# Gate columns of the mLSTM group as eight extra columns of its value projection, and small passes moved between VectorE, ScalarE and GpSimd

## The reference, cut to what matters

```python
# mLSTM: 4 gates of each kind are columns 1280..1287 of w_in
q, k, v, o, i_pre, f_pre = split_cols(p, (GW, GW, GW, GW, nh, nh))
log_i = gate(i_pre, i_bias)
bcum  = cumsum(log_sigmoid(gate(f_pre, f_bias)))
# S5: complex diagonal state, per state p
mag, ang = exp(lr * step), li * step
ab_re, ab_im = mag * cos(ang), mag * sin(ang)
den   = lr * lr + li * li
co_re = ((ab_re - 1.0) * lr + ab_im * li) / den
co_im = (ab_im * lr - (ab_re - 1.0) * li) / den
# RWKV-7: key scaled by its gate
k = k * (1.0 + (a - 1.0) * k_a)
```

## Time and profile before

| | |
|---|---|
| median of 3 runs | 480.02 us |
| the profiled execution: its time, and its span from first to last instruction | 479.55 us, 477.7 us |
| PE busy | 467.7 us, 98% |
| DVE busy | 345.0 us, 72% |
| ACT busy | 272.5 us, 57% |
| POOL busy | 108.4 us, 23% |
| mean granted TensorE clock | 0.997 |
| DVE busy from 60 to 120 us | 58.7 us |
| first read of `xres` (DVE, L2146) | 211.2 us |
| weight load, median from issue to landing | 4.8 us |

### The profile page before, as it was taken

One profiled execution on the slowest core, in us unless ns is written; L12 is line 12 of the kernel. 1 busy time (PEld: TensorE's weight loads), 2 busy tenths in 40 slices (PEclk: granted clock), 3 DMA queues, 4 the chain that ended last, 5 costly groups with the idle time before them and its releaser, 6 DMA issues.

```text
span 477.7 us, 8231 instructions
## 1 busy us (share of the span) xinstructions
PE 467.7 (98%) x3330; PEld 407.4 (85%) x3330; DVE 345.0 (72%) x482; ACT 272.5 (57%) x448; POOL 108.4 (23%) x75
## 2 busy tenths in 40 slices
PE   9999999999999999999999999999999999999995
PEld 6999888988889887889998887888888888888884
DVE  3999999999789987887564747766767777642234
ACT  5778884426334557589366657555555555553332
POOL 0005327793566610000000000000000000444450
PEclk9999999999999999999999999999999999999998
DMA  7884428221411226274633622565554555455502
GB/s 268 331 326 158 173 89 325 69 95 55 149 56 54 90 89 263 90 263 165 233 101 145 238 91 88 184 227 197 206 200 177 176 185 189 169 206 213 185 0 89
DMA packets 12697, 78.91 MB, mean 165 GB/s; under 512 B 1487, under 2 KB 2164, under 8 KB 4084
## 3 DMA queue, kind: packets, MB, share of 16 engines
q1 hardware_dynamic: 12660, 78.39, 45.4%
HBM read 77.33 MB, written 1.84 MB: 166 GB/s over the span
## 4 chain that ended last, share of the span: by engine, by line
PE 74%; DVE 4%; issue 0%; DVEq 0%; ACT 0%
PE bank L415 73%; DVE h L1956 1%; DVE wm_rest L386 1%; DVE wk_rest L386 0%; PE bank L943 0%; PE bank L974 0%; DVE arena L1978 0%; PE bank L653 0%; DVE arena L1899 0%; DVE arena L1969 0%; DVE arena L1979 0%; DVE arena L1927 0%; DVE arena L1925 0%; DVE arena L1898 0%; DVE xres L2146 0%
## 5 line engine op out<-in xcount | busy, mean ns | idle before, releaser
L415 PE MATMUL bank<-h,w_high 128*128 128x512 f32 (+1 forms) x392 | 120.7, 373 | 0.0
L380 ACT ACTIVATE w_high<-ring 128x1024 fp32r<-128x1024 f32 x63 | 66.2, 1058 | 61.2 <-PE bank L415 57.0
L386 DVE TENSOR_TENSOR w_rest<-ring,w_high 128x1024 fp32r<-128x1024 f32 x51 | 63.2, 1245 | 48.8 <-ACT w_high L380 48.6
L415 PE MATMUL bank<-h,w_rest 128*128 128x256 f32 x320 | 89.6, 280 | 0.0
L415 PEld LDWEIGHTS bank<-h,w_high 128*128 128x128 f32 x392 | 68.8, 188 | 13.6 <-issue 0.5
L386 POOL TENSOR_TENSOR w_rest<-ring,w_high 128x1024 fp32r<-128x1024 f32 x7 | 16.8, 2400 | 256.5 <-ACT w_high L380 256.5
L415 PEld LDWEIGHTS bank<-h,w_rest 128*128 128x128 f32 x320 | 60.5, 189 | 0.0
L386 DVE TENSOR_TENSOR w_rest<-third_slot,w_high 128x1024 fp32r<-128x1024 f32 x27 | 32.7, 1223 | 27.3 <-ACT w_high L380 27.2
L415 PE MATMUL bank<-arena 64*64 64x64 f32 (+6 forms) x786 | 50.2, 253 | 2.2 <-POOL arena L1116 1.1
L415 PEld LDWEIGHTS bank<-arena 64*64 64x64 f32 (+3 forms) x786 | 41.8, 144 | 11.3 <-issue 4.6
L415 PE MATMUL bank<-h,we_high 128*128 128x256 f32 x256 | 47.2, 287 | 1.2 <-DVE we_rest L386 0.8
(11 more groups left out here) (346 smaller groups left out, 1038.7 us busy)
## 6 DMA issues: line engine op xcount, KB each, us to landing
ring<-weights SPq DMA_DIRECT2D x49, 1024.0 KB, 4.8
third_slot<-weights SPq DMA_DIRECT2D x15, 1024.0 KB, 4.8
gain<-gains SPq DMA_DIRECT2D x3, 512.0 KB, 5.8
cst<-consts SPq DMA_DIRECT2D x1, 1216.0 KB, 8.6
par<-params SPq DMA_DIRECT2D x1, 1168.0 KB, 10.6
kx<-x_t SPq DMA_DIRECT2D x2, 512.0 KB, 5.7
ring<-weights SPq DMA_DIRECT2D x2, 512.0 KB, 6.6
vx<-mem_t SPq DMA_DIRECT2D x1, 1024.0 KB, 10.0
```

The costliest lines, as they stand in the source:

```text
L380: nc.scalar.activation(split_half(i)[0], raw_half(i), ACT.Copy).then_inc(S["w_high"], 1)
L386: e.tensor_tensor(rest_, raw_half(i), high.bitcast(F32), ALU.subtract).then_inc(rest_done(i)[0], 1)
L415: return nc.tensor.matmul(out_, lhsT, rhs, start=start, stop=stop, skip_group_check=True)
```

## The change

- **Gates.** `w_gate` shrinks from 36 to 8 columns per tile. Buffer pairs `we2` and `we3` are 264 columns wide; their last 8 columns hold the split gate weights, made once by two small ACT operations (high) and two small DVE operations (rest). ml_v's two token halves go to banks 6 and 2 with 264 columns each; ACT's `gated_values` copies 8 gate columns and 256 values of each, scaled. PE transposes the gate columns (two transposes into bank 7) between the two halves of ml_o, after waiting until ACT has moved both. The float32 products, L1793 and the gates' `x_scale` go.
- **Phases.** The eight first passes move from DVE to ACT, in groups of 3, 3 and 2 among the highs. `highs(9)` comes ahead of the table load, `highs(15)` ahead of the next one; `rests(9)` comes ahead of the subtraction L1782, `rests(15)` ahead of `conv_back` of ml_q.
- **S5 coefficients** go to POOL, ahead of `s5_readout`; the denominator and its reciprocal stay on DVE, earlier.
- **Key scale** `Kh` (L1854) and **nM** (L1947) move from DVE to ACT.
- **Banks and buffers.** ml_o uses bank 0; the A products' banks are reordered (the last in bank 0, no bank twice); BKt and Vt swap places. The second `prs` lies on `xres`, so `rotate_back(1)` no longer waits for `h_rest`, and the load of `xres` moves from slot 12 to slot 22, after `s5_y`.

```diff
-GATES = 36
+GATES = 2 * NH
+GATE_ROWS = 36
-        prs = [v4(pr_, 2, T), v4(flat(vx), 2, T)]
+        prs = [v4(pr_, 2, T), v4(flat(xres), 2, T)]
+        gate_cols = v3(R_[:, 0:2 * 64], 64)
-            w_early = [pair(stage, f"we{i}", HALF, 256) for i in range(HALF_BUFS)]
+            w_early = [pair(stage, f"we{i}", HALF, 256) for i in range(2)]
+            w_gated = [pair(stage, f"we{i}", 4 * (256 + GATES), 256 + GATES) for i in range(2, HALF_BUFS)]
+            w_early += [[x[:, :, 0:256] for x in w] for w in w_gated]
@@ tensor
+            def values_and_gates(n, names, banks, act):
+                for name, b in zip(names, banks):
+                    pe_open(pe, name, b)
+                pe.wait_ge(S["gate_split"], 4)
+                for j in range(2):
+                    i = 2 * n + j
+                    wait_rest(pe, i)
+                    for m in range(2):
+                        o = bank[banks[m]][:, 0:256 + GATES]
+                        for k in range(4):
+                            kt = 4 * j + k
+                            last = mm3(o, [x[:, kt, m * P:(m + 1) * P] for x in act],
+                                       [x[:, k, :] for x in w_gated[j]], kt == 0, kt == KD - 1)
+                        if j == 1 and m == 0:
+                            last.then_inc(full[banks[0]], 1)
+                    used(last, i, names[1] if j else None)
-            o = pe_open(pe, "gates", 2)
-            pe.wait_ge(S["gate_gain"], 1)
-            for k in range(KD):
-                last = mm(o[0:GATES, 0:T], v3(prm("w_gate"), GATES)[:, k, :], hT[:, k, :], k == 0, k == KD - 1)
-            last.then_inc(full[2], 1)
-            split_values(7, "ml_v", 0, h_split)
-            split_channel_major(8, "ml_o", 1, h_split)
+            values_and_gates(7, ("ml_v0", "ml_v1"), (6, 2), h_split)
+            split_channel_major(8, "ml_o", 0, h_split, None, (0,))
+            o = pe_open(pe, "gates", 7)
+            moved(pe, "ml_v0")
+            moved(pe, "ml_v1")
+            for m in range(2):
+                last = nc.tensor.transpose(o[0:GATE_ROWS, m * P:(m + 1) * P], gate_cols[:, m, 0:GATE_ROWS], const("ident"))
+            last.then_inc(full[7], 1)
+            split_channel_major(8, "ml_o", 0, h_split, None, (1,))
-                    b = (4, 5, 6, 7, 0, 2, 3, 6)[i]
+                    b = (4, 5, 1, 7, 6, 2, 3, 0)[i]
@@ sync
+                if n == S_V6:
+                    wait_full(sp, "s5_y")
                     sp.dma_start(xres, x_rows.rearrange("(m p) c -> p m c", p=P)).then_inc(S["xres_in"], 16)
@@ gpsimd
+            s5_coefficients()
             s5_readout()
-                if q == 1:
-                    pool.wait_ge(S["h_rest"], 4)
@@ scalar
+            def gated_values(m, name):
+                o = wait_full(act, name)
+                act.wait_ge(S["rstd_col"], 1)
+                act.wait_ge(S["zeros_ready"], 2)
+                a.activation(v3(gate_cols[:, m, :], 32)[:, :, 0:NH], v3(o[:, 256:256 + GATES], NH), ACT.Copy,
+                             scale=rstd_col[:, m:m + 1])
+                a.activation(mlv[:, m, :], o[:, 0:256], ACT.Copy, scale=rstd_col[:, m:m + 1]).then_inc(free_of(name), 1)
+            def phase(i):
+                a.activation(sin[:, i, :], const("time"), ACT.Copy, scale=frac[:, i:i + 1]).then_inc(S["phase"], 1)
+            for i in range(3):
+                phase(i)
             highs(7)
             shifted("rw_k", 1)
             highs(8)
+            for i in range(3, 6):
+                phase(i)
+            highs(9)
+            for i in range(6, 8):
+                phase(i)
+            for j in range(2):
+                a.activation(w_gated[j][0][:, :, 256:256 + GATES], raw_gates(j), ACT.Copy).then_inc(S["gate_split"], 1)
+            highs(15)
+            moved(act, "rw_a")
+            for j in range(2):
+                e = a.activation(Kh[:, j, :], ab[:, j, :], ACT.Identity, bias=one_ka[:, j:j + 1], scale=half_ka[:, j:j + 1])
             highs(H_MID + 2)
             act.wait_ge(S["rw_E"], 1)
-            project_values("ml_v", mlv)
+            gated_values(0, "ml_v0")
+            gated_values(1, "ml_v1")
+            o = wait_full(act, "gates")
-            act.wait_ge(S["ml_rows"], 3)
+            act.wait_ge(S["ml_row_step"], 3)
+            a.activation(rows[2][0:NH, :], rows[0][0:NH, :], ACT.Copy, scale=-1.0).then_inc(S["ml_rows"], 1)
@@ vector
-            for i in range(8):
-                last = v.tensor_scalar(sin[:, i, :], const("time"), frac[:, i:i + 1], None, ALU.mult)
-            last.then_inc(S["theta"], 1)
+            rests(9)
+            dve.wait_ge(S["phase"], 8)
             v.scalar_tensor_tensor(sin, cos, ROUND, sin, ALU.subtract, ALU.subtract).then_inc(S["theta"], 1)
-            rests(9)
-            v.tensor_tensor(w_gate, w_gate, spread(prm("pre_mix"), GATES), ALU.mult).then_inc(S["gate_gain"], 1)
+            for j in range(2):
+                dve.wait_ge(S["gate_split"], j + 1)
+                high, rest_ = (x[:, :, 256:256 + GATES] for x in w_gated[j])
+                v.tensor_tensor(rest_, raw_gates(j), high.bitcast(F32), ALU.subtract).then_inc(S["gate_split"], 1)
+            rests(15)
-            for j in range(2):
-                last = v.tensor_scalar(Kh[:, j, :], ab[:, j, :], half_ka[:, j:j + 1], one_ka[:, j:j + 1], ALU.mult, ALU.add)
-            x_scale("gates", GATES, 1)
-            v.tensor_scalar(nM, lf, -1.0, None, ALU.mult).then_inc(S["ml_rows"], 1)
```

More of the change, by code:

```diff
@@ L320, in wait_slot @@
             return slot(n)
-        SCALED = ["rw_wag", "rw_k", "rw_r", "rw_v", "ml_q", "ml_k", "gates", "ml_o"]
+        SCALED = ["rw_wag", "rw_k", "rw_r", "rw_v", "ml_q", "ml_k", "ml_o"]
         def scaled(eng, name):
@@ L844, in _ @@
             moved(pe, "qk3")
-            moved(pe, "ml_v")
+            moved(pe, "ml_v1")
             attend("num", 2, mlv, E)
@@ L1132, in s5_readout, with s5_coefficients @@
                 g.tensor_scalar(c_im, xr, -1.0, None, ALU.mult).then_inc(S["s5_c"], 1)
+            def s5_coefficients():
+                lr, li, cos1, sin1 = prm("lam_re"), prm("lam_im"), cos[:, :, 1], sin[:, :, 1]
+                pool.wait_ge(S["sincos"], 3)
+                pool.wait_ge(S["s5_step"], 2)
+                g.tensor_tensor(s8b, mag, cos1, ALU.mult)
+                g.tensor_tensor(s8c, mag, sin1, ALU.mult).then_inc(S["s5_co_step"], 1)
+                pool.wait_ge(S["s5_co_step"], 2)
+                g.tensor_scalar(s8b, s8b, -1.0, None, ALU.add).then_inc(S["s5_co_step"], 1)
+                pool.wait_ge(S["s5_co_step"], 3)
+                g.tensor_tensor(co_re, s8b, lr, ALU.mult)
+                g.tensor_tensor(s8a, s8c, li, ALU.mult)
+                g.tensor_tensor(co_im, s8c, lr, ALU.mult)
+                g.tensor_tensor(frn, s8b, li, ALU.mult).then_inc(S["s5_co_step"], 1)
+                pool.wait_ge(S["s5_co_step"], 4)
+                g.tensor_tensor(co_re, co_re, s8a, ALU.add)
+                g.tensor_tensor(co_im, co_im, frn, ALU.subtract).then_inc(S["s5_co_step"], 1)
+                pool.wait_ge(S["s5_co_step"], 5)
+                pool.wait_ge(S["s5_den"], 2)
+                g.tensor_tensor(co_re, co_re, den8, ALU.mult)
+                g.tensor_tensor(co_im, co_im, den8, ALU.mult).then_inc(S["s5_co"], 1)
             pool.wait_ge(S["sq_m_ready"], 1)
             sum_tiles(pool, g, sq_m, "mem_summed")
+            s5_coefficients()
             s5_readout()
@@ L1364, in _ @@
             a.activation(rwE[:, 2], Gp, ACT.Exp, scale=-1.0).then_inc(S["rw_E"], 1)
[L1365 to L1368, removed]
             s5_driving(0)
@@ L1373, in _ @@
             act.wait_ge(S["rw_E"], 1)
-            project_values("ml_v", mlv)
+            gated_values(0, "ml_v0")
+            gated_values(1, "ml_v1")
+            o = wait_full(act, "gates")
+            a.activation(rows[0][0:NH, :], o[32:32 + NH, 0:T], ACT.Identity,
+                         bias=prm("f_bias", NH)).then_inc(S["ml_gate"], 1)
+            a.activation(rows[1][0:NH, :], o[0:NH, 0:T], ACT.Identity, bias=prm("i_bias", NH)).then_inc(free_of("gates"), 1)
             act.wait_ge(S["ml_gate"], 1)
@@ L1739, in _ @@
             dve.wait_ge(S["theta"], 3)
+            lr, li = prm("lam_re"), prm("lam_im")
+            v.tensor_tensor(den8, lr, lr, ALU.mult)
+            v.tensor_tensor(s8b, li, li, ALU.mult).then_inc(S["s5_den"], 1)
+            dve.wait_ge(S["s5_den"], 1)
+            v.tensor_tensor(den8, den8, s8b, ALU.add).then_inc(S["s5_co_step"], 1)
+            dve.wait_ge(S["s5_co_step"], 1)
+            v.reciprocal(den8, den8).then_inc(S["s5_den"], 1)
             def mix(n, name):
@@ L1776, in _ @@
             rests(8)
+            dve.wait_ge(S["consts_in"], 16)
             for i in range(8):
@@ L1852, in _ @@
             k2 = rwM[:, 2:4, :]
-            for j in range(2):
-                last = v.tensor_scalar(Kh[:, j, :], ab[:, j, :], half_ka[:, j:j + 1], one_ka[:, j:j + 1], ALU.mult, ALU.add)
```

(7 more changed lines are left out.)

53 lines of the change are left out of this document (18 added, 35 removed).

## The result

The changed kernel takes 484.44 us (median of 5 runs; 484.03 for the four without the one named below) against 479.83 us of the kernel before on the same chip, a ratio of 1.0088 for those four (95% interval 1.0073 to 1.0103). On a second chip it was 484.01 against 479.77, 1.0082 (1.0065 to 1.0099). Forecast were 475.9 us and a range of 473.6 to 478.8. One profiled execution of the changed kernel took 1174 us, with TensorE's products at about twice their time (776 instead of 379 ns for those of h with `w_high`); it is left out, and all that follows reads the ordinary execution of the second chip (484.17 us, span 482.4).

What follows compares the result with a forecast made beforehand. The prediction took PE, busy 467.7 of 477.7 us, as the bound. Its terms, 0.2 + 3.1 + 0.4 - 0.7 + 0.3 + 1.1 - 1.0 + 0.7 = 4.1 us less, gave 475.9 us, range 473.6 to 478.8.

Steps and rivals of the forecast that it cites:

- The collision, -1.0: Before 119.40 us, freed `rotate_back(1)` on POOL runs beside DVE's memory rests 4 to 7 and costs 1.0 us.
- the alternating lock: Rival with a late slot 9: POOL-DVE collision costs 2.5, transposes wait 1.5; 1.8 us less, 478.2 us; chance 0.20.
- The issue before level five, +0.7: At 125.37 us PE waits for POOL's mask; made some 4 us early, it ends that wait and gains 0.7 us.
- Gates, +3.1: PE's float32 gate products go, 3.58 us, less 0.2 for 264-column products and 0.3 for transposes: 3.1 us gained.
- The wait at the transposes, -0.7: Near 67 us PE waits for ACT's `gated_values`, held by slot 9's landing and highs: 0.7 us lost.
- ACT from 22 to 50 us, +0.2: ACT's idle time takes most of the phase passes, gate splits and `Kh`; of half 8's 0.8 us gap 0.2 is kept.
- ml_o's bank, +0.4: At 68 us PE's wait for the bank that ml_k holds goes, since ml_o uses bank 0: 0.4 us gained.
- the last A bank, +0.3: At 78 us PE's wait before the last A product goes, since no bank is used twice: 0.3 us gained.
- DVE after ml_k, "3.4 us sooner": Without `Kh` and the gates' scale on DVE, `rw_tilde` comes about 3.4 us sooner and keeps up with PE.
- nM, +1.1: nM leaves DVE for ACT: 1.19 us less 0.1 of overlap, so DVE gains 1.1 and is 4.4 ahead at 113 us.
- the five kinds of wait: PE's waits from 20 to 180 us, given as 3.3 us together; with 0.7 of issue, 4.0 us of gaps.
- the rival in which all gaps close: No wait at the transposes and no collision: 7.1 us less at most, 473.3 to 474.5 us; chance 0.14.

Runs made afterwards that it cites:

- b3_both: The changed kernel with 224 unused columns behind the parameters (addresses of before) and the `h_rest` wait of `rotate_back(1)` put back; 477.80 us, ratio 0.9955.
- b1_pad: The changed kernel with 224 unused columns behind the parameters, so later buffers lie at their addresses of before; 481.46 us, ratio 1.0032.
- b2_h_rest: The changed kernel with only the wait of `rotate_back(1)` for `h_rest` put back; 479.67 us, ratio 0.9999.
- d4_phases_dve: b3_both with the eight first phase passes back on DVE; 478.34 us, ratio 0.9972.
- d2_free_rotation: The kernel before with `rotate_back(1)` freed of its `h_rest` wait, the second `prs` on `xres` and its later load, nothing else; 484.21 us, ratio 1.0093.
- d3: b3_both with POOL's mask of level five ahead of `rotate_back(1)` instead of behind it; 477.83 us, ratio 0.9961.
- f1: The changed kernel padded, level-four mask behind memory rests 0 to 3, level-five mask behind rests 4 to 7 and ahead of `rotate_back(1)`; 477.73 us, ratio 0.9958.
- a1_after: The changed kernel once more, unchanged; 484.01 us, ratio 1.0082.

## Why the prediction was wrong

It failed at one term that was mis-sized, "I take 1.0" for what `rotate_back(1)` meets (3.4 us, and 1.28 us of clock behind it), and at one that it lacked, the addresses (2.0 us). Without the two (b3_both) the change gains 2.2 us by the ratio, 1.7 by the spans (476.0 against 477.7). The forecast's own terms for such a kernel, without the collision and with the issue back, come to 4.1 + 1.0 - 0.7 = 4.4, so the remaining ones were too high as well. Point by point, on b3_both where not said otherwise:

- **The collision, -1.0 (bounds 0 to 3.5).** The mechanism was named and the place was right; the size was 3.4 us on DVE (5.08 - 1.66), the upper bound. That the sum of five times 0.7 comes so near is luck: four operations met POOL, and three of them lost 1.0 us each and the last 0.4. "Back-to-back DVE operations mostly keep going once started" did not hold here. The 0.7 us of the earlier trace rows was one meeting, and I multiplied it by an uncertain share of five operations; what counts is how often the two engines meet, and which of them has to wait. Here it was DVE, with operations (474 ns) far shorter than POOL's (1.3 us alone). The same meeting went the other way at 101 us in the kernel before, where three long DVE operations with operands in SBUF alone kept their 1.21 us and POOL's product beside them took 5.39; its timeline, POOL and then DVE (the first of the three is in the earlier trace rows):

```profile
101.42 5.39 POOL L1149 TENSOR_TENSOR arena<-arena 128x512 f32<-128x512 f32 x1
...
103.31 1.21 DVE L386 TENSOR_TENSOR wk_rest<-ring,wk_high 128x1024 fp32r<-128x1024 f32 x1
104.44 1.21 DVE L1969 SCALAR_TENSOR_TENSOR arena<-arena 128x1024 f32<-128x1024 f32 x1
```

  What decides between the two ways is not shown. The Trainium skill ("SBUF — State Buffer", SBUF: two separate sides) says that such operations exclude each other for the whole instruction. This trace agrees: the level updates, with one operand in a bank of PSUM, kept their 0.40 us beside POOL at 114 us, and the memory rests, with SBUF operands alone, did not. The half's rest at 115.14, two SBUF inputs as well, kept its 1.22 us, and there it was POOL's product that took 2.25.
- **What the wait does to PE's clock.** No term. A wait of 3.70 us brought 1.2 GHz behind it and 1.28 us more (1.05 in b1_pad, where the products took 56.77). A much shorter one can do it too: in b2_h_rest and in d4_phases_dve the clock fell at 112.0 us, behind waits of 1.39 and 1.37 us, and in b3_both, behind the same 1.39, it did not. Windows of b2_h_rest and then of b3_both:

```profile
112.00:114.00 2.00, 2.00 (x12) 2.00 (x11) 2.00 (x6) 0.00 (x0) 0.00 (x0) 0.50 0.00 0
```

```profile
112.00:114.00 2.00, 2.00 (x19) 2.00 (x18) 2.00 (x5) 0.00 (x0) 0.00 (x0) 1.00 0.00 0
```

  There it cost little, since the waits of 0.27 and 0.71 us behind it closed. What decides whether it falls is open. The rival "the alternating lock" priced the collision at 2.5; by itself, with the clock, it is 4.5 (d2_free_rotation).
- **The issue before level five, +0.7.** Right in the changed kernel, where it went, paid for by the collision. In b3_both it is back (0.71). The mask and the memory rests want POOL and DVE at one time; d3 and f1 show that either order costs about the same.
- **Addresses, no term.** 2.0 us. The diff shows the constant `GATES` shrink a parameter block at the front of memory; that everything behind it moves was to be seen, that it has a price was not to be had from any row of before.
- **Gates, +3.1.** Right on PE. Products of 264 columns last 286 and 282 ns (high and rest) against 285 and 283 for 256 columns, and from the first start of ml_v's 48 to the last it is 5.77 us (59.56 to 65.33 in a1_after) against 5.72 (61.76 to 67.48 before), so my 0.2 for them is nearer 0. No float32 product of 36 rows is left.
- **The wait at the transposes, -0.7.** Measured 0.61 in a1_after, 0.50 in b3_both. The size was right and the reason half: slot 9 was issued at 61.10 instead of 61.55, not at 59.7, and PE came later too. The rows of PE's waits before 80 us, timeline of b3_both:

```profile
10.37 0.51 PE L423 MATMUL bank<-h,we_high 128*128 128x256 f32 x2 [0.74 <-DVE we_rest L394]
...
38.65 0.51 PE L423 MATMUL bank<-h,we_high 128*128 128x256 f32 x2 [0.83 <-DVE we_rest L394]
54.59 0.50 PE L423 MATMUL bank<-h,we_high 128*128 128x256 f32 x2 [0.37 <-DVE we_rest L394]
68.57 0.38 PE L783 MATMUL bank<-cst,arena 128*36 128x128 f32 x2 [0.50 <-ACT arena L1293]
75.75 1.75 PE L423 MATMUL bank<-arena 64*128 64x256 f32 x36 [0.29 <-ACT arena L1472]
```

- **ACT from 22 to 50 us, +0.2.** Half 8's gap of 0.76 closed, and 0.83 opened at half 9 and 0.37 at half 13: 0.4 lost, not 0.2 gained. I had followed halves 8 to 10 and stopped there. The passes on ACT are not what opened the two gaps: with them on DVE (d4_phases_dve) they are 0.80 and 0.37. What did is open. (The 0.74 at 10.37 is no part of it: the same gap is 0.29 and 0.32 in a1_after and missing in others; it varies from run to run.)
- **ml_o's bank, +0.4, and the last A bank, +0.3.** The first is gone. At the second an equal wait (0.29, for ACT's L1472) took its place.
- **DVE after ml_k, "3.4 us sooner".** It is 1.3: `rw_tilde` starts at 67.88 against 69.21. DVE was 2.3 us ahead when the key product began and 1.2 when it ended, with POOL's readout beside it; DVE of b3_both:

```profile
60.52 1.23 DVE L1925 SCALAR_TENSOR_TENSOR arena<-arena 128x512 f32<-128x512 f32 x1
61.67 1.22 DVE L1926 TENSOR_TENSOR arena<-arena 128x512 f32<-128x512 f32 x1
```

  Before, they came when the readout was nearly over and took 0.69 each (62.81 to 64.10). The eleven coefficient operations that I had called free ran from 50.77 to 56.2 us on POOL in a1_after (0.2 to 1.2 us each, not the 0.15 to 0.2 that I took from DVE's) and pushed the readout from 54.96 to 56.24 (55.82 in b3_both). That alone did not make the meeting: before, too, the readout was running at 60.5 us, where the key product now begins.
- **nM, +1.1.** DVE lost the operation. At 103 us DVE is 2.7 ahead (103.01 against 105.75), and by the end of memory rests 0 to 3 only 1.7: they ran beside POOL's `rotate` and masks and took 3.45 us against 2.43 before. From there to the end it stays at 1.7.

DVE of b3_both at this place:

```profile
105.62 2.17 DVE L394 TENSOR_TENSOR wm_rest<-ring,wm_high 128x1024 fp32r<-128x1024 f32 x1
107.72 3.45 DVE L2021 SCALAR_TENSOR_TENSOR h<-vx,par,h 128x256 fp32r<-128x256 f32 x4
```

So b3_both is 2.4 ahead at the A products (71.74 against 74.16; forecast 3.3) and 1.7 from 111 us on (forecast 4.4 at 113). In the changed kernel three losses, at the key product, at rests 0 to 3 and at rests 4 to 7, look like one mechanism: DVE came earlier, or POOL did, and they met. Only the third was tested by a run that removes it.

One sum of the prediction is wrong and does not enter the forecast: the five kinds of wait of the earlier trace rows come to 0.8 + 0.4 + 0.3 + 0.4 + 0.9 = 2.8 us and not 3.3, so 3.5 us of gaps were to be had up to 126 us, and the rival in which all gaps close has 6.6 us less at most and not 7.1.

The signs that I had named came out so: no wait on `h_rest`, no issue, the ACT wait and no dear 264-column products as said; A products 1.9 us sooner (72.28) and not 3; the memory-key half at 121.5 and not 116; PE busy 467.7 and not 463 to 465; and "a DVE stretch before 119 longer by over 2 us", a sign for wrong, was there with 3.4.

## What to carry to other kernels

A wait between DVE and POOL that looks like a mere claim on a buffer can be what keeps them apart. Before it is removed, price the meeting as if the short operations came no closer together than the long ones beside them, as an upper bound (here they started 1.4 us apart instead of 0.4), and add the clock if PE will stand still as long as here. After a change in the size of any early buffer, look at the mean time of untouched products in a late stage. If it moved, pad the buffer to its old size before judging the rest of the change.

## What was unexpected of the hardware

- Float32r products with 512 columns took 391 or 399 ns, and the same 872 products 165.28 or 167.29 us, by a shift of their buffers by 128 bytes. Shifts of 32 and of 512 bytes did nothing. Moving either operand's buffers without the other's cost 1.45 to 1.48 us.
- Four DVE operations of 128x256 lasted 5.08 us beside POOL's products of 128x512 and a mask, and 1.66 without them. POOL's four products took only 0.3 us more than before (6.30 against 6.00). Beside three DVE operations of 128x1024 it was POOL that waited: 5.39 us for a product of 1.3.
- A wait of 3.70 us took PE's clock from 2.4 to 1.2 GHz for some 3 us of full work behind it and cost 1.05 to 1.28 us. Of two waits of 1.39 us at the same place, that of b2_h_rest was followed by 1.2 GHz as well and that of b3_both was not.
